# A decoder trunk on one core: projections of the next head pair placed between the attention steps of the present one, the two heads of a pair in halves of the TensorE array

## The chip, the cores and the metric

The kernel runs on one core of one Trainium2 chip, as one program. A core has TensorE (matmuls, results in PSUM, 8 banks of 128 x 512 words), VectorE, ScalarE, GpSimd and a DMA queue on SyncE. The metric is the time of one execution on the device in microseconds (us); the shown time is a median of three runs.

## The reference, cut to what matters

512 tokens, width 1024, two layers. Each layer is a mixer (three kinds of causal attention, six heads of 64 each), merged by gates, and then a feed-forward part with 16384 experts and product keys. Only the mixer's first half is touched:

```python
xn = rms_norm(h, norm1_g[l])
proj = xn @ w_in                       # qa ka va  qb kb vb  f  qc kc vc  gates
# branch 0 (A): dilated windows: the three patterns are one softmax with a mask of log counts
# branch 1 (B): softmax(q.k / 8 + cum[t] - cum[s]) over s <= t,  cum = cumsum(log_sigmoid(f + b))
# branch 2 (C): window of 128, 6 query heads on 2 key heads, a sink in the denominator
oa, ob, oc = attention of each branch, per head
merged = sum over branches of sigmoid(gate_b) * (o_b @ w_br_b)
h = h + merged @ w_out
```

Attention works in blocks of 128 queries; a query block `qi` sees the key blocks `blocks(br, qi)`: 1, 2, 3, 4 of them in branches 0 and 1, and 1, 2, 2, 2 in branch 2.

## The kernel before, in words

**Streams and splits.** All weights come as chunks of 128 x 2048 words (1 MB) through two slots: a load (L325), ScalarE copies the high part (`split_hi`, L458) and VectorE subtracts the rest (`split_lo`, L743), and TensorE multiplies high by high, high by low and low by high (`product`, L1153 to L1155). `ahead(p, s)` on both engines means the split of the chunk after this one. A slot is split again only when TensorE has used it up (`w_used`).

**Order of a layer's mixer.** Normalise and transpose x; two chunks for the keys and values that branch 2 shares (`kv`, evicted by L504); then three head pairs `hp`, one after the other; then the merge: 24 chunks, each with 8 products for a gate and 3 for a branch; then the output projection.

**One head pair.** Four chunks give the projections of the pair: 64 products, each 3 matmuls over 452 columns. Between them VectorE rotates queries and keys (L816 to L822), and VectorE and ScalarE make the forget gate's logarithm (L517, L518; it needs another ScalarE table than the exponential) and the cumulated sum. Then 24 transposes (L1227) give `qT` and `kT`. `qT` is kept once per head, with the other head's 64 rows zero (set by GpSimd once in a layer), so that logits are matmuls of all 128 rows. GpSimd copies the pair's shared keys and values into `proj` (L410).

**The attention of a pair.** 24 units (branch, head, query block) in a pipeline written out by hand with four logit buffers. A unit: logits on TensorE (L1244; branch 1 adds L1246), mask and maximum on VectorE (L877), negated maximum (L882, L884), exponential on ScalarE (L545), reciprocal and normalisation on VectorE (L893, L894), transposes of the probabilities on TensorE (L1257), copy to SBUF on ScalarE (L557), values on TensorE (L1267), which form 128 output columns of which one head's 64 are kept. TensorE issues logits three units ahead; the transposes have two banks. Outputs are split in high and low (L563, L796) for each branch and head. All engines execute in order, with waits on semaphores.

## Time and profile before

| | us |
|---|---|
| median of 3 runs (3490.7 to 3494.0) | 3491.5 |
| the profiled execution | 3496.1 |
| its span in the trace | 3494.3 |

| stage of layer 0 | us from the span's start |
|---|---|
| x, shared keys and values | 0 to 38.4 |
| three head pairs | 38.4 to 279.6 |
| merge, output projection | 280 to about 484 |
| the feed-forward part | to about 1750 |

Layer 1 repeats this. The page gives busy shares of the whole span; what an engine waits for is read from the chain of waits and from the timeline of a stage.

### The profile page before, as it was taken

What the parts mean: (1) busy time and instruction counts of PE and PEld (TensorE: products, weight loads), DVE (VectorE), ACT (ScalarE), POOL (GpSimd) and SP (SyncE); (2) the same over time, 40 slices, a digit from 0 to 9 for tenths busy, and PEclk for the clock granted to TensorE, in tenths of its full rate; (3) what the DMA queues carried; (4) which work ended last, traced back from release to release, by engine and by line L of the source; (5) the groups of instructions that cost most, each with busy time, mean ns of one, the idle gap of its engine ahead of it and who ended that gap; (6) DMA issues with size and microseconds to landing.
All of it is one profiled execution on the core that took longest, in us unless ns stands there. A gap on an engine that the chain in (4) does not pass through costs nothing.

```text
span 3494.3 us, 53359 instructions
## 1 busy us (share of the span) xinstructions
PE 3421.8 (98%) x18272; PEld 3003.5 (86%) x18272; DVE 2677.5 (77%) x5087; ACT 1642.3 (47%) x2531; POOL 1109.9 (32%) x701
## 2 busy tenths in 40 slices
PE   7999999999999999999999999999999999999998
PEld 6888778999999987777788887789999998878777
DVE  5665448999997688888866644399999967888887
ACT  5664333457775333333356643334577753333333
POOL 1000003673333354444200000137633333544442
PEclk9999999999999999999999999999999999999999
DMA  4112322569999999999721133225799999999996
GB/s 148 48 48 106 135 102 85 178 232 369 370 369 388 367 376 360 370 374 378 293 85 49 48 121 132 104 83 190 259 371 367 364 388 366 385 357 380 374 369 248
DMA packets 226906, 885.59 MB, mean 253 GB/s; under 512 B 20752, under 2 KB 70304, under 8 KB 178000
## 3 DMA queue, kind: packets, MB, share of 16 engines
q1 hardware_dynamic: 121136, 478.99, 37.1%
q0 software_dynamic: 83648, 304.09, 23.1%
q10 hardware_dynamic: 21984, 100.94, 7.1%
q8 instruction: 54, 0.88, 0.1%
q14 instruction: 84, 0.69, 0.1%
HBM read 781.17 MB, written 102.76 MB: 253 GB/s over the span
## 4 chain that ended last, share of the span: by engine, by line
PE 75%; DVE 10%; DMA 6%; issue 5%; ACT 4%; ACTq 0%; DVEq 0%; SPq 0%
PE bank L1153 18%; PE bank L1155 17%; PE bank L1154 17%; PE bank L1420 13%; DMA raw<-in_stream 5%; PE bank L1384 5%; DVE lo L743 3%; DVE h L1055 3%; PE bank L1267 2%; DVE act_in L1106 1%; ACT hi L458 1%; ACT w_hi L706 1%; PE bank L1244 1%; PE bank L1257 1%; PE bank L1333 1%
## 5 line engine op out<-in xcount | busy, mean ns | idle before, releaser
L743 DVE TENSOR_TENSOR lo<-raw,hi 128x2048 fp32r<-128x2048 f32 x304 | 696.5, 2291 | 335.6 <-ACT hi L458 333.4
L1153 PE MATMUL bank<-xT_hi,hi 128*128 128x352 f32 (+1 forms) x2688 | 924.7, 344 | 4.5 <-DVE lo L743 2.4
L1154 PE MATMUL bank<-xT_lo,hi 128*128 128x352 f32 (+1 forms) x2688 | 910.9, 339 | 0.0
L1155 PE MATMUL bank<-xT_hi,lo 128*128 128x352 f32 (+1 forms) x2688 | 910.4, 339 | 0.0
L458 ACT ACTIVATE hi<-raw 128x2048 fp32r<-128x2048 f32 x324 | 620.0, 1914 | 408.8 <-PE bank L1420 172.4
L1420 PE MATMUL bank<-hi,w_hi 128*128 128x512 f32 x1536 | 612.6, 399 | 10.8 <-DVE w_lo L1108 10.4
L1420 PE MATMUL bank<-hi,w_lo 128*128 128x512 f32 x1536 | 608.8, 396 | 0.0
L1420 PE MATMUL bank<-lo,w_hi 128*128 128x512 f32 x1536 | 608.8, 396 | 0.0
L1153 PEld LDWEIGHTS bank<-xT_hi,hi 128*128 128x128 f32 x2688 | 506.2, 188 | 34.6 <-issue 7.2
L447 POOL DMA_INDIRECT rows<-in_v_rows,ids x256 | 387.4, 1513 | 467.0 <-DVE h L1055 383.8
L1155 PEld LDWEIGHTS bank<-xT_hi,lo 128*128 128x128 f32 x2688 | 505.4, 188 | 25.9
L1154 PEld LDWEIGHTS bank<-xT_lo,hi 128*128 128x128 f32 x2688 | 505.8, 188 | 24.3
L447 POOL DMA_INDIRECT rows<-in_u_rows,ids x256 | 327.4, 1279 | 536.7 <-DVE act_row L1052 450.3
L1420 PEld LDWEIGHTS bank<-hi,w_hi 128*128 128x128 f32 x1536 | 289.2, 188 | 94.2 <-DVE w_lo L1108 25.5
L1420 PEld LDWEIGHTS bank<-hi,w_lo 128*128 128x128 f32 x1536 | 289.3, 188 | 70.5
L1420 PEld LDWEIGHTS bank<-lo,w_hi 128*128 128x128 f32 x1536 | 289.4, 188 | 68.9
L1055 DVE SCALAR_TENSOR_TENSOR h<-rows,w_row,h 128x1024 f32<-128x1024 f32 x256 | 328.3, 1283 | 16.6
L706 ACT ACTIVATE w_hi<-act_in 128x768 fp32r<-128x768 f32 x128 | 108.4, 847 | 487.7 <-DVE act_in L1106 484.4
L1052 DVE CUSTOM_DVE_ANT_0 rows<-rows,x_row 128x1024 f32<-128x1024 f32 x256 | 300.4, 1221 | 0.1
L1108 DVE TENSOR_TENSOR w_lo<-act_in,w_hi 128x768 fp32r<-128x768 f32 x128 | 122.7, 958 | 126.6 <-ACT w_hi L706 126.6
L435 POOL TENSOR_TENSOR lo<-raw,hi 128x1024 fp32r<-128x1024 f32 x64 | 201.0, 3154 | 45.1 <-ACT hi L638 45.0
L1089 DVE TENSOR_SCALAR onehot<-iota_sb,idx1T,gT 128x128 f32<-128x128 f32 x768 | 202.9, 365 | 0.0
(213 smaller groups left out, 4608.2 us busy)
## 6 DMA issues: line engine op xcount, KB each, us to landing
raw<-in_stream SPq DMA_DIRECT2D x356, 1024.0 KB
act_d<-act_s ACTq DMA_DIRECT2D x128, 384.0 KB
gate_d<-gate_s ACTq DMA_DIRECT2D x24, 2048.0 KB
act_in<-act_d SPq DMA_DIRECT2D x128, 384.0 KB
gate_in<-gate_d SPq DMA_DIRECT2D x28, 1536.0 KB
gate_in<-gate_d SPq DMA_DIRECT2D x16, 384.0 KB
rows<-in_u_rows,ids POOLq DMA_INDIRECT x256
rows<-in_v_rows,ids POOLq DMA_INDIRECT x256
```

What stands on the lines that cost most here:

```text
L435: pool.tensor_tensor(lo[s][:, half], raw[s][:, half], hi[s][:, half].bitcast(F32), ALU.subtract).then_inc(lo_done if i else lo0_done, 1)
L447: pool.indirect_dma_start(rows[:, N % NR], None, a["u_rows" if n < E + P else "v_rows"], bass.IndirectOffsetOnAxis(which, 0)).then_inc(row ...
L458: act.activation(hi[s][:], raw[s][:], ACT.Copy).then_inc(hi_done, 1)
L743: dve.tensor_tensor(lo[s][:], raw[s][:], hi[s][:].bitcast(F32), ALU.subtract).then_inc(lo_done, 1)
L1052: last = dve.tensor_tensor_reduce(row, row, x_row[:], 1.0, 0.0, ALU.mult, ALU.add, act_row[:, k])
L1055: last = dve.scalar_tensor_tensor(out=h[:, ROWED], in0=row, scalar=w_row[:, k], in1=h[:, ROWED], op0=ALU.mult, op1=ALU.add)
L1089: last = dve.tensor_scalar(o[:, r, 0], iota[:], idx1T[:, t], gT[:, t], ALU.is_equal, ALU.mult)
L1153: pe.matmul(dst, a_[0], b_[0], start=first, stop=False)
L1154: pe.matmul(dst, a_[0], b_[1], start=False, stop=False)
L1155: return pe.matmul(dst, a_[1], b_[0], start=False, stop=last)
L1384: last = pe.matmul(ps[4 + slot][:, tile(r)], o[:, 1], o[:, 0], start=True, stop=True)
L1420: last = pe.matmul(ps[2 * tt + nh][:], wp[:, s, i, tile(tt)], v[vp][:, 2 * i + nh], start=False, stop=False)
```

## The change

- The projections of pair 0 run alone as before. The 64 products of the next pair are then dealt out over 25 slots that stand between the attention steps of the present pair (`slot`, `proj_groups`), two or three products each. In the last pair the slots carry 16 gate products of the merge's first two chunks instead (`gate_groups`).
- The two heads of a pair are one step: 12 steps `w` instead of 24 units. Each head's logits are a matmul of its 64 rows of `qT` and `kT`, head 0 in the upper rows of the array and head 1 in the lower, into two banks; values use 64 columns of the array for each head, into one bank. `qT` is kept once for both; the zeroing of halves is gone.
- Banks: logits 0 and 1, transposes one bank (2) for both heads in turn, outputs one bank (3), projections 4 to 7. Two logit buffers per head instead of four for all. TensorE issues logits two steps ahead.
- ScalarE and VectorE do the splits of the next pair's chunks at steps 0, 3, 6 and 9, evictions at 4 to 6 and 10 to 12, the rotation (in halves of two query tiles) at 7, 8, 10, 11, the forget gate at 1 to 4. Negated maxima, reciprocals and sink terms are done once for both heads, and the output's high and low parts for both heads at once.
- Before pair 0's projections TensorE now waits for the shared keys and values to be evicted (`kv_ev`; before: ahead of the third chunk). GpSimd copies the values of branches 0 and 1 into `v_ab`; shared keys and values are read in place.

```diff
+STEPS = [(br, qi) for br in (0, 2, 1) for qi in range(NT)]
+NW = len(STEPS)
+TURN_BANK, O_BANK, PROJ_BANK = 2, 3, 4
+PRE_SLOTS = 3
+SLOTS = PRE_SLOTS + 2 * NW
+FILLED = SLOTS - 2
+PROJ_GROUPS = PROJ_CHUNKS * NT * NK // 2
+EARLY_GATES = 2
+SPLIT_AT = {0: 0, 3: 1, 6: 2, 9: 3}
+EVICT_AT = {4: [(0, 0), (0, 1)], 5: [(0, 2)], 6: [(0, 3)], 10: [(1, 0)], 11: [(1, 1)], 12: [(1, 2), (1, 3)]}
+ROPE_AT = (7, 8, 10, 11)
+F_EXP_AT, F_SUM_AT, CUM_HI_AT, CUM_LO_AT = 1, 2, 3, 4
```

ScalarE's steps:

```diff
+                    for w in range(NW + 1):
+                        if w < NW:
+                            br, qi = STEPS[w]
+                            nk = len(blocks(br, qi)) * P
+                            act.wait_ge(lg_done, NW * b + w + 1)
+                            for hh in range(2):
+                                u = 2 * w + hh
+                                done = act.activation(lg[:, w % 2, hh, 0:nk], lg[:, w % 2, hh, 0:nk], ACT.Exp,
+                                                      bias=nmx[:, u:u + 1], accum_out=den[:, u:u + 1])
...
+                        if w == F_EXP_AT:
                             link = Chain(act, f_act, 2 * b, 2)
                             act.wait_ge(f_x, b + 1)
                             link(act.activation(fg[:, 1], fg[:, 1], ACT.Exp))
                             link(act.activation(fg[:, 1], fg[:, 1], ACT.Ln, bias=one[0:2, 0:1]))
...
+                        for hh in range(2 if w > 0 else 0):
+                            v = w - 1
+                            nk = len(blocks(*STEPS[v])) * P
+                            act.wait_ge(tr_done, 2 * (NW * b + v) + hh + 1)
+                            if hh == 0:
+                                act.wait_ge(pv_done, NW * b + v + 1)
+                            act.activation(pT[:, hh, 0:nk], ps[TURN_BANK][:, 0:nk], ACT.Copy).then_inc(pt_done, 1)
+                            if hh == 0:
+                                tasks(hp, w, last)
+                        if w == 0:
+                            tasks(hp, w, last)
+                        if not last:
+                            for r, tt in EVICT_AT.get(w, ()):
+                                proj_evict(b + 1, r, tt)
```

VectorE's steps:

```diff
+                    for w in range(NW):
...
+                        for hh in range(2):
+                            u = 2 * w + hh
+                            if w >= 2:
+                                dve.wait_ge(tr_done, 2 * (NW * b + w - 2) + hh + 1)
+                            wait_alone(dve, s_ps, 2 * (NW * b + w) + hh + 1, dve_passed)
+                            dve.tensor_tensor_reduce(lg[:, w % 2, hh, 0:nk], ps[hh][:, 0:nk], m, SCALE, -3e38, ALU.add, ALU.max,
+                                                     mx[:, u:u + 1]).then_inc(mx_link, 1)
+                        dve.wait_ge(mx_link, 2 * (NW * b + w) + 2)
...
+                        if w in SPLIT_AT and not last:
+                            c = SPLIT_AT[w]
+                            ahead(lp + KV_CHUNKS // 2 + (hp + 1) * (PROJ_CHUNKS // 2) + c // 2, c % 2)
+                        if w == 0 and last:
+                            ahead(lp + P_MRG, 0)
...
+                        dve.wait_ge(ex_done, NW * b + w + 1)
...
+                        den_chain(dve.reciprocal(rden[:, pair], den[:, pair]))
+                        for hh in range(2):
+                            u = 2 * w + hh
+                            dve.tensor_scalar(lg[:, w % 2, hh, 0:nk], lg[:, w % 2, hh, 0:nk], rden[:, u:u + 1], None,
                                               ALU.mult).then_inc(pn_done, 1)
+                        if w >= NT + 1 and (w - NT - 1) % NT == 0:
+                            o_split_lo(b, hp, (w - NT - 1) // NT)
```

TensorE's logits, values and order:

```diff
+                        for hh in range(2):
+                            of = slice(hh * DH, hh * DH + DH)
+                            done = pe.matmul(dst[hh], qT[br][of, tile(qi)], kT[br][of, keys], start=True, stop=br != 1)
...
+                                done = pe.matmul(ps[O_BANK][of, tile(qi)], v, pT[:, hh, tile(n)],
+                                                 start=n == 0, stop=n == len(bl) - 1)
...
+                    def slot(i):
+
+                        total = EARLY_GATES * NK if last else PROJ_GROUPS
+                        first, end = (min(total, -(-total * n // FILLED)) for n in (i, i + 1))
+                        if last:
+                            gate_groups(first, end, b)
+                        else:
+                            proj_groups(hp + 1, first, end, b)
+
+                    logits(0)
+                    slot(0)
+                    slot(1)
+                    logits(1)
+                    slot(2)
+                    for w in range(NW):
+                        if w >= 1:
+                            values(w - 1)
+                        turn(w, 0)
+                        slot(PRE_SLOTS + 2 * w)
+                        turn(w, 1)
+                        if w + 2 < NW:
+                            logits(w + 2)
+                        slot(PRE_SLOTS + 2 * w + 1)
+                    values(NW - 1)
+
+                pe.wait_ge(kv_ev, l + 1)
+                proj_groups(0, 0, PROJ_GROUPS)
+                for hp in range(HP):
+                    attention(hp, hp == HP - 1)
```

`turn(w, 1)` waits for the copy of `turn(w, 0)` out of the one bank (`pt_done`), `values(w)` for both copies, and the first values of a branch for the low part of the branch before (`o_lo`).

## Rows read from the trace of the kernel before

**Rows 1.** The page: busy time of each engine, and the chain that ended last, by engine.

```profile
PE 3421.8 (98%) x18272; PEld 3003.5 (86%) x18272; DVE 2677.5 (77%) x5087; ACT 1642.3 (47%) x2531; POOL 1109.9 (32%) x701
...
PE 75%; DVE 10%; DMA 6%; issue 5%; ACT 4%; ACTq 0%; DVEq 0%; SPq 0%
```

**Rows 2.** Windows of layer 0: busy us, instructions, PE clock, DMA.

```profile
core 0: us, PE busy (x) PEld busy (x) DVE busy (x) ACT busy (x) POOL busy (x), PEclk, DMA share, GB/s
...
38.40:78.54 40.14, 39.98 (x198) 36.18 (x197) 22.21 (x20) 17.57 (x23) 3.14 (x2) 1.00 0.37 130
...
78.54:119.03 40.49, 37.50 (x243) 29.15 (x242) 32.18 (x137) 31.86 (x94) 0.00 (x0) 1.00 0.00 1
...
280.00:372.00 92.00, 92.00 (x401) 74.82 (x400) 42.73 (x35) 35.04 (x30) 0.00 (x0) 1.00 0.37 134
```

**Rows 3.** The chain, start and us: last value products of four pairs.

```profile
118.12 1.16 PE bank L1267 x8
...
198.39 1.16 PE bank L1267 x8
...
1853.06 1.16 PE bank L1267 x8
...
1933.74 1.16 PE bank L1267 x8
```

**Rows 4.** The chain, first pair: spacing of attention matmuls.

```profile
89.50 0.44 PE bank L1257 x4
...
90.61 0.86 PE bank L1244 x2
...
91.58 0.89 PE bank L1267 x8
...
113.81 0.23 PE bank L1246
```

**Rows 5.** Timeline, start and us: one unit of four blocks on VectorE and ScalarE.

```profile
114.96 0.15 DVE L884 TENSOR_SCALAR nmx<-mx 128x1 f32<-128x1 f32 x1
...
115.15 0.72 ACT L545 ACTIVATE lg<-lg,nmx 128x512 f32<-128x512 f32 x1 [0.69 <-DVE nmx L884]
...
116.00 0.16 DVE L893 RECIPROCAL rden<-den 128x1 f32<-128x1 f32 x1 [0.36 <-ACT lg L545]
...
116.20 0.48 DVE L894 TENSOR_SCALAR lg<-lg,rden 128x512 f32<-128x512 f32 x1
```

**Rows 6.** Groups by form, 38.4 to 280 us: count, busy us, mean ns, idle.

```profile
L545 ACT ACTIVATE lg<-lg,nmx 128x512 f32<-128x512 f32 x12 | 8.7, 722 | 7.4 <-DVE nmx L884 7.4
...
L545 ACT ACTIVATE lg<-lg,nmx 128x128 f32<-128x128 f32 x18 | 7.2, 398 | 0.6 <-DVE nmx L882 0.5
...
L877 DVE CUSTOM_DVE_ANT_0 lg<-bank,mask_b 128x512 f32<-128x512 f32 x6 | 4.2, 692 | 2.3 <-PE bank L1257 2.3
...
L877 DVE CUSTOM_DVE_ANT_0 lg<-bank,mask_b 128x128 f32<-128x128 f32 x6 | 1.7, 285 | 0.0
...
L557 ACT ACTIVATE pT<-bank 128x512 f32<-128x512 f32 x12 | 7.1, 593 | 1.6 <-PE bank L1257 1.5
```

**Rows 7.** Timeline: one weight chunk split, high half and low half.

```profile
121.31 1.92 ACT L458 ACTIVATE hi<-raw 128x2048 fp32r<-128x2048 f32 x1
...
123.26 2.29 DVE L743 TENSOR_TENSOR lo<-raw,hi 128x2048 fp32r<-128x2048 f32 x1 [2.41 <-ACT hi L458]
```

**Rows 8.** Timeline: the forget gate's logarithm and its table.

```profile
71.22 1.28 ACT L518 ACT_TABLE_LOAD   x1
...
72.51 0.72 ACT L518 ACTIVATE fg<-fg,one 2x512 f32<-2x512 f32 x1
```

**Rows 9.** Timeline: the shared keys and values leave their banks.

```profile
38.60 2.32 ACT L504 ACTIVATE kv<-bank 128x256 f32<-128x256 f32 x8 [3.78 <-PE bank L1155]
```

**Rows 10.** Windows at the start of the span, as rows 2.

```profile
21.70:24.40 2.70, 0.00 (x0) 0.00 (x0) 2.70 (x3) 2.70 (x6) 0.00 (x0) 1.00 0.00 0
...
26.80:30.20 3.40, 3.40 (x18) 3.40 (x17) 3.40 (x5) 0.98 (x1) 0.93 (x2) 0.51 0.32 135
```

More of the change, by code:

```diff
@@ L106 @@
 FIRST_PAIR, REST_PAIR = 0, 8
-ZEROED = 7
 TWO_PI = 2 * np.pi
@@ L567, in _, with o_hi_split @@
+                def o_hi_split(b, hp, g):
+                    act.wait_ge(pv_done, NW * b + NT * g + NT + 1)
+                    act.activation(oT_hi[:, bass.ds(hp * 3 + STEPS[NT * g][0], 1), :].rearrange("p o t -> p (o t)"),
+                                   ps[O_BANK][:], ACT.Copy).then_inc(o_hi, 1)
+                with act.Fori(0, HP - 1) as hp:
+                    attention(hp, False)
+                attention(HP - 1, True)
+                for j in range(NK // M_BLOCKS):
                     for m in range(3 * M_BLOCKS):
@@ L902, in _ @@
+                with dve.Fori(0, HP - 1) as hp:
+                    attention(hp, False)
+                attention(HP - 1, True)
+                for j in range(NK // M_BLOCKS):
                     for m in range(3 * M_BLOCKS):
@@ new lines, in proj_groups @@
+                        if g % 16 == 0:
+                            take(lp + KV_CHUNKS // 2 + hp * (PROJ_CHUNKS // 2) + c // 2, s)
+                        if beside is not None and c == 0 and k == 0:
+                            bank_free(beside, tt)
+                        if c == 2 and k == 0:
+                            pe.wait_ge(proj_ev, 2 * NT * b + tt + 1)
+                        last = product(ps[PROJ_BANK + tt][:, 0:PROJ_COLS], at(xT, s * NK // 2 + k, tile(tt)),
+                                       at(chunk(s, PROJ_COLS, NK // 2), k), s == 0 and k == 0, s == 1 and k == 3)
@@ new lines, in proj_groups, with gate_groups @@
+                        if g % 16 == 15:
+                            last.then_inc(w_used, 1)
+                        elif s == 1 and k == 3:
+                            last.then_inc(proj_ps, 1)
+                def gate_groups(first, end, beside):
+                    for g in range(first, end):
+                        m, k = g // NK, g % NK
+                        if k == 0:
+                            take(lp + P_MRG, m)
+                            bank_free(beside, m)
+                        product(ps[4 + m][:], at(chunk(m, P, NK + HP), k), at(xT, k), k == 0, k == NK - 1)
@@ new lines, in logits, with turn @@
+                        for hh in range(2 if br == 1 else 0):
+                            pe.matmul(dst[hh], select[:, hh], cum[:, keys], start=False, stop=True).then_inc(s_ps, 1)
+                    def turn(w, hh):
+                        n = 2 * (NW * b + w) + hh
+                        pe.wait_ge(pn_done, n + 1)
+                        if w == hh == 0:
+                            pe.wait_ge(heads_dve, 3 * b + 2)
+                        else:
+                            pe.wait_ge(pt_done, n)
+                        for i in range(len(blocks(*STEPS[w]))):
+                            done = pe.transpose(ps[TURN_BANK][:, tile(i)], lg[:, w % 2, hh, tile(i)], ident[:])
+                        done.then_inc(tr_done, 1)
```

435 lines of the change are left out of this document (187 added, 248 removed).

## The prediction

> **What bounds the kernel now.** I read the page first, then windows by stage, then the chain and the timeline of one head pair. TensorE is busy 98% of the span and carries 75% of the chain [rows 1], so a gain must take work or idle time from TensorE. The change touches three head pairs and the start of the merge in each layer. Two successive pairs of layer 0 end 80.3 us apart, two of layer 1 80.7 [rows 3]. The window of pair 0 divides at 78.5: about 39.4 us of products (64 x 3 matmuls, 0.205 each), all of them dense, then 40.5 us of attention, in which neither VectorE (32) nor ScalarE (32) is full [rows 2]. What TensorE really needs there comes from spacings, because busy time counts the drain of a lone matmul. A transpose takes 0.11, a value product (two records) 0.22, a logits product 0.86 for 512 columns and its decay term 0.23 [rows 4]. A pair has 28 transposes of heads and gates and 54 of probabilities (9.0), 6912 logit columns (11.6), 2560 columns with decay (1.2) and 54 value products (12.0): 33.8 us. The pair's 80.3 less 39.4 and 33.8 leaves **7.1 us of idle TensorE**. That is all that better cover can bring, 43 us for six pairs. If both heads' matmuls ran at once, values would halve (6 us) and logits lose a quarter, since only the second record of head 0 and the first of head 1 can overlap (2.9): 8.9 a pair, 53 in all.
>
> **What the change adds: one ring.** Before, VectorE put the next unit's reduction ahead of waiting for an exponential, with four logit buffers. Now each step does, in order, two reductions, a negation, a wait for both exponentials, one reciprocal, two normalisations; the next reduction stands behind that wait. For four blocks: reductions 2 x 0.73, 0.19 to the exponential, 2 x 0.72, 0.32 to the first normalisation, 2 x 0.40: 4.2 us, from the starts in [rows 5] and the means in [rows 6], less 0.1 where neighbours overlap. One block gives 2.5 in the same way; two and three lie between (3.0, 3.6); the sink terms of branch 2 add 0.6. Twelve steps: 2 x 13.3 + 13.9 = **40.5 us** serial.
>
> Into that ring the change puts more, in the two pairs that carry projections. A split costs 1.95 on ScalarE and then 2.2 on VectorE [rows 7]; VectorE takes it before it waits for the exponential, ScalarE after a copy, so the whole 4.2 stands between exponential and normalisation at steps 0, 3, 6 and 9: 17.8 with the copies. The gate's logarithm (exponential 0.6, table 1.28, logarithm 0.72) [rows 8] now stands in ScalarE's queue at step 1, ahead of the copy that frees the one transpose bank; the way back to the exponential's table costs another 1.28, mostly waited for anyway. Low parts, sums and rotation not hidden by an exponential: about 3. VectorE starts 4.6 after the last values (low part 0.65, three head copies, two gate operations), and the last step needs 3.9 for two turns through one bank and its values. The ring alone: 4.6 + 40.5 + 17.8 + 4 + 3.9 = **71 us**. TensorE alone: 39.4 + 33.8 = 73 without overlap of the heads, 64 with. Two chains of nearly equal length with only two steps of look-ahead don't hide each other wholly.
>
> **Laid out step by step** from the end of the values before, with TensorE's order as the diff gives it and a group of three matmuls at 0.615, TensorE waits: 1.8 at the first transpose (it has 5 us of slots, the ring with the split takes 11); 3.4 at the second (the logarithm stands before its copy; one slot of 1.85 covers); 0.8 and 1.4 around the split at step 3, where the copy for the second head stands behind the next step's exponentials, which stand behind the late normalisation; 0.3 and 1.8 at step 6; 1.5 and 0.5 at step 9, where the values of branch 1 need the low part that VectorE does after the split; 1.2 in the last step, whose slots are empty. Sum 12.7: the pair takes 33.8 + 39.4 + 12.7 = **85.9 us**, if the halves of the array bring nothing, and 80.5 if they overlap as above (a part of the 8.9 turns into waits for the ring). No row shows a matmul in a part of the array. Nothing excludes a loss either: every step goes four times between shapes, and a last matmul shows 1.16 where spaced ones show 0.89 [rows 3, 4], so an emptied array costs at most 0.27, 13 us a pair for 48 changes. I take half of the overlap's gain: **83.2**.
>
> The Trainium skill ("TensorEngine Tiling (Array Packing)", Key Properties) says that different tiles can execute in parallel, and in the same list that changing the tiling mode drains the engine, which speaks against this order of steps. By the first alone a pair would take 80.5, by both about 84; no run here shows either yet.
>
> **The last pair of a layer** has 16 gate products of 3 x 0.23 (401 matmuls in the 92 us of the merge's window [rows 2]) in its slots, 11.0 us, and one split. TensorE needs 44.8, the ring 4.6 + 40.5 + 4.2 + 4 + 3.9 = 57. But now the look-ahead is the limit: logits of step w+2 stand behind the second transpose of w, that behind a copy, that behind the exponentials of w+1. From one exponential to the next but one this takes a copy (0.3 to 0.6) [rows 6], a transpose, the logits (0.4 to 2.2), reductions and exponentials; laid out it comes to 66.8, and 64 with overlap: **65.4**, against 40.9 before.
>
> **The smaller parts.** The wait for `kv_ev` ahead of pair 0's first product: before, TensorE went on while ScalarE evicted from 38.60 for 2.32 us [rows 9]. Nothing stands behind it: +2.5 a layer. VectorE's rotation of the shared keys moves with it and stays hidden. At the merge's start the gate products are gone that covered the third chunk's split: branch products of the two chunks take 4.2, sigmoid and split end at 7.1: +2.9, and -11.0 for the products moved. Removed memsets, GpSimd's copies and the lesser zero rows were on no chain; its new copy of the values (about 2 us) has 19 us. Loads (two in 10 us) are as many and have a step of slack.
>
> **The clock.** After 2.7 us without a matmul TensorE ran 3.4 us at half its clock, that is 1.2 GHz, some 2.4 us later [rows 10]. The waits of 3.4 us in two pairs, and two of over 4 us at the start of the last, may do that; a drop costs up to 1.7. I take about one in a layer: +1.5.
>
> **Sum.** A layer's pairs took 240.8. Now 39.4 + 2.5 + 2 x 83.2 + 65.4 + 2.9 - 11.0 + 1.5 = 267.1, +26.3; both layers +52.6. The span would be 3546.9 for 3494.3; the profiled execution (3496.1) lies 0.1% above the median of the runs, 3491.5, so I put the median at **3544 us**.
>
> **Rivals.** (1) *The tasks hide.* If splits and logarithm fell where engines wait anyway and the ring stayed at its own length, a pair would take 72 and the last 54: 39.4 + 2.5 + 144 + 54 + 2.9 - 11.0 = 231.8 a layer, 3473 in all, **faster**. It decides below 76 us a pair. For it: TensorE's products cover 3.2 us of each step. Against it: all four engines' orders are fixed, and the waits above follow from them. If tiles overlapped and all waits vanished too, the limit would be near 3395; hardly likely. Chance 0.19. (2) *Tiles cost.* No overlap and a drain of half of 0.27 at each change, a third of it in waits: 90 a pair, 71 the last, 3580. Chance 0.16. (3) *The gains meet the waits*: full overlap, and a third of the laid-out waits: some 75 a pair and 58 the last, 3493. Chance 0.07. That the shapes don't take effect as array parts is the no-overlap case, 63 us over: 3555, within the forecast. Forecast, 3515 to 3565: 0.58.
>
> **How the numbers follow.** A measurement of this kernel can tell 0.2% from no change, 7 us. The range takes in the forecast, (3) and most of (1) and (2): 3472 to 3588. Faster 0.20, within 0.2% 0.06, slower 0.74.
>
> **What would show it.** The start of the second attention should come some 83 us after the first; TensorE should idle 3 us before the second transpose, released by ScalarE's copy, with a table load ahead of it; VectorE should wait for ScalarE's high part at steps 0, 3, 6, 9; the last pair should take 60 to 70 us and TensorE be about two thirds busy in it; value products of two heads should be spaced by 0.11 to 0.22. I am wrong if a pair with projections takes under 77 us, or if the last pair's steps run at 3.4 us as before; then the ring overlaps in a way that I haven't seen.

## The result and the profile after

The changed kernel takes **3558.1 us** (median of four runs, 3555.0 to 3562.6) against 3491.1 on the same chip: a ratio of 1.0195, 95% interval 1.0177 to 1.0212, so 67 us slower. Its profiled execution took 3557.6, with a span of 3555.8, 61.5 more than the span of before.

First the page of the changed kernel: busy time and the chain that ended last.

```profile
PE 3411.0 (96%) x18272; PEld 2948.2 (83%) x18272; DVE 2650.8 (75%) x4974; ACT 1603.2 (45%) x2463; POOL 1103.8 (31%) x683
...
PE 73%; DVE 11%; issue 7%; ACT 6%; DMA 3%; ACTq 0%; DVEq 0%; SPq 0%
```

As many matmuls as in [rows 1] are busy for 11 us less, though the span is 61 longer: the busy share falls from 98% to 96%, and what is new is idle TensorE.

The stages of layer 0, on the timeline of TensorE (start, duration, line, [idle before]):

```profile
40.14 0.47 PE L1186 MATMUL bank<-hi,xT_hi 128*128 128x452 f32 x1 [2.50 <-ACT kv L504]
...
81.06 1.47 PE L1279 MATMUL bank<-ident_sb,proj 128*128 128x128 f32 x12
...
165.87 1.53 PE L1279 MATMUL bank<-ident_sb,proj 128*128 128x128 f32 x12
...
251.74 1.53 PE L1279 MATMUL bank<-ident_sb,proj 128*128 128x128 f32 x12
...
319.93 1.09 PE L1332 MATMUL bank<-pT,v_ab 128*64 128x128 f32 x16 [0.69 <-ACT pT L560]
...
328.39 0.79 PE L1186 MATMUL bank<-xT_hi,hi 128*128 128x512 f32 x1 [2.96 <-DVE lo L764]
```

Attention begins with the head transposes (L1279). The pairs that carry projections take 84.8 and 85.9 us (80.3 before, [rows 3]), the last one 69.3 to the end of its values at 321.0. In layer 1 they take 84.8, 84.9 and 71.5. Attention of layer 0 ended at 279.6 before, so it ends 41.4 later. Layer 1's head transposes come 33.7 later (1846.84 for 1813.11), and up to 2.5 of that is the second layer's own wait for `kv_ev`: from the merge on 10.2 is given back, 11.0 less 3.0 of it by the moved gate products and the wait at 328.39. The matmuls from 328.97 on are 0.43 apart, at half clock; those from 331.9 on are 0.23 apart.

Windows of the same stages (length, busy us and instructions by engine, granted clock):

```profile
81.06:166.40 85.34, 74.76 (x444) 55.73 (x443) 45.53 (x130) 42.69 (x101) 1.32 (x2) 0.96 0.14 50
166.40:251.74 85.34, 74.35 (x437) 54.71 (x434) 45.86 (x131) 42.13 (x100) 0.76 (x1) 0.94 0.14 50
251.74:320.90 69.16, 48.16 (x296) 28.50 (x294) 33.01 (x116) 32.41 (x88) 1.04 (x1) 0.88 0.05 16
320.90:412.00 91.10, 88.14 (x379) 71.49 (x376) 43.45 (x37) 34.23 (x30) 0.00 (x0) 0.98 0.37 127
```

TensorE is idle for some 11 us in each of the first two, where it was idle 3.0 in the 40.5 of [rows 2], and for 21 in the last pair. The granted clock was 1.00 in all of this stage before. A mean of 0.96, 0.94 and 0.88 between levels of 1.0 and 0.5 is 7, 10 and 17 us at half clock (1.2 GHz). In layer 1 the means are 0.98, 0.98 and 0.82: 3, 3 and 26 us.

What TensorE waits for in the first of these stretches, then in the last (engine, line waited for: us in total, times, longest):

```profile
PE bank L1314 <- ACT pT L560: 4.6, 4, 1.6
PE bank L1314 <- DVE lg L919: 3.4, 3, 2.0
PE bank L1332 <- DVE oT_lo L815: 1.8, 1, 1.8
PE bank L1332 <- ACT pT L560: 0.7, 1, 0.7
...
PE bank L1314 <- ACT pT L560: 13.0, 11, 3.4
PE bank L1314 <- DVE lg L919: 5.9, 2, 4.7
```

L1314 is the transpose of the probabilities. It waits either for the normalisation (L919) or for the copy (L560) that frees the one transpose bank for the second head: 8.0 us with projections, 18.9 in the last pair. L1332 are the value products; with their waits the first stretch has 10.5 us.

### The profile page after: what moved, and what is told of

Its sections match the earlier page's. It is cut to its first block, busy times and chain, and to the rows that moved or that the text cites. A ratio compares the mean times of both kernels' runs of the same rounds, so it can differ in the third digit from the quotient of the medians.

```text
span 3555.8 us, 52652 instructions
## 1 busy us (share of the span) xinstructions
PE 3411.0 (96%) x18272; PEld 2948.2 (83%) x18272; DVE 2650.8 (75%) x4974; ACT 1603.2 (45%) x2463; POOL 1103.8 (31%) x683
## 4 chain that ended last, share of the span: by engine, by line
PE 73%; DVE 11%; issue 7%; ACT 6%; DMA 3%; ACTq 0%; DVEq 0%; SPq 0%
PE bank L1186 17%; PE bank L1187 17%; PE bank L1188 17%; PE bank L1503 14%; PE bank L1467 5%; DVE h L1087 4%; DVE lo L764 3%; DMA raw<-in_stream 3%; ACT hi L458 2%; DVE act_in L1138 1%; ACT w_hi L727 1%; PE bank L1314 1%; PE bank L1332 1%; ACT lg L537 1%; PE bank L1300 1%
## 5 line engine op out<-in xcount | busy, mean ns | idle before, releaser
L1188 PE MATMUL bank<-xT_hi,lo 128*128 128x352 f32 (+1 forms) x2688 | 912.0, 339 | 0.0
L447 POOL DMA_INDIRECT rows<-in_v_rows,ids x256 | 395.0, 1543 | 451.9 <-DVE h L1087 362.2
L1188 PEld LDWEIGHTS bank<-xT_hi,lo 128*128 128x128 f32 x2688 | 507.0, 189 | 26.8
```

What stands on the lines that cost most here:

```text
L447: pool.indirect_dma_start(rows[:, N % NR], None, a["u_rows" if n < E + P else "v_rows"], bass.IndirectOffsetOnAxis(which, 0)).then_inc(row ...
L1188: return pe.matmul(dst, a_[1], b_[0], start=False, stop=last)
```

## The experiments

Each ratio is to the kernel before on the same chip (3489 to 3490 us); the time beside it is a median, and differences are to the 3558.1 of the change, whose own chip had 3491.1 for the kernel before. Two stage times recur, both of layer 0: *pairs* are the distances between the transposes of the shared keys in successive pairs (84.9 and 85.9 in the changed kernel), *last* is from there to the end of the layer's values (67.9).

| kernel | us | pairs | last |
|---|---|---|---|
| changed | 3558.1 | 84.9, 85.9 | 67.9 |
| full shapes | 3577.3 | 88.1, 86.5 | 71.7 |
| reductions ahead | 3576.0 | 87.5, 86.1 | 74.5 |
| logarithm late | 3545.2 | 83.1, 82.4 | 69.2 |
| products early | 3546.7 | 83.2, 82.2 | 68.0 |
| filler in the last pair | 3551.1 | 84.9, 84.9 | 65.9 |
| no interleaving | 3676.4 | 115.4, 114.2 | 68.7 |
| the same, full shapes | 3664.5 | 110.1, 109.4 | 71.3 |
| split late | 3571.4 | 88.7, 88.7 | 68.9 |
| all mended | 3560.1 | 88.0, 88.5 | 64.4 |
| mended, split kept | 3541.4 | 82.2, 83.5 | 66.9 |

**1. The heads' matmuls in full shapes.**

```diff
-    done = pe.matmul(dst[hh], qT[br][of, tile(qi)], kT[br][of, keys], start=True, stop=br != 1)
+    done = pe.matmul(dst[hh], qT[br][:, tile(qi)], kT[br][:, keys], start=True, stop=br != 1)
...
-    v = v_ab[:, kb, br * P + hh * DH:br * P + hh * DH + DH]
-    done = pe.matmul(ps[O_BANK][of, tile(qi)], v, pT[:, hh, tile(n)],
-                     start=n == 0, stop=n == len(bl) - 1)
+    v = v_ab[:, kb, br * P:br * P + P]
+    done = pe.matmul(ps[O_BANK][:, tile(qi)], v, pT[:, hh, tile(n)],
+                     start=n == 0 and hh == 0, stop=n == len(bl) - 1 and hh == 1)
```

> The changed kernel with its order kept, but logits and values as full 128 x 128 array shapes (same count and columns). It computes something else: each head's logits are the sum over both heads, and the values of both heads are added. In the trace of the changed kernel four value products of a head pair are spaced 0.216 us per key block plus 0.16 once, where full shapes take 0.44 per block: the parts save TensorE about 7.8 us a pair. Theory (the ring of reductions, exponentials and normalisations sets the pace, the parts' gain goes mostly into waits): a pair with projections goes from 85.3 to 88 to 90, the last from 69 to about 71, the median from 3558 to 3575 to 3590. Rival 1 (TensorE sets the pace and all of the gain counts): +47, 3605. Rival 2 (changing the shape of the array costs more than the overlap gives): at or under 3558.

Measured: 3577.3, ratio 1.026 (1.0243 to 1.0277), 19 us more, as the first theory has it. Each head's logits and values hold the other head's as well here, so only times can be compared. What the parts save is read from the same step in the changed kernel and in this one, where a row's next row starts when the array is free:

```profile
161.00 0.36 PE L1188 MATMUL bank<-hi,xT_lo 128*128 128x452 f32 x1
161.29 0.88 PE L1332 MATMUL bank<-pT,v_ab 128*64 128x128 f32 x12
162.10 0.66 PE L1314 MATMUL bank<-ident_sb,lg 128*128 128x128 f32 x4
...
164.84 1.09 PE L1332 MATMUL bank<-pT,v_ab 128*64 128x128 f32 x16 [0.69 <-ACT pT L560]
```

```profile
162.34 0.37 PE L1188 MATMUL bank<-hi,xT_lo 128*128 128x452 f32 x1
162.54 1.50 PE L1332 MATMUL bank<-pT,v_ab 128*128 128x128 f32 x12
163.88 0.60 PE L1314 MATMUL bank<-ident_sb,lg 128*128 128x128 f32 x4
```

Four more value records (a key block of both heads) take 0.22: 0.81 for twelve up to the next row, 1.03 for sixteen (the next row there is L1279 at 165.87). In full shape a block of *one* head takes that ([rows 4]). So the two heads overlap wholly. But the visit to the other shape costs time, and not only inside it: the product before it (L1188) holds the array for 0.29 and not 0.20, and the transposes behind it last 0.06 longer. From the start of the record before a visit to the start of the second record behind it, at full clock and without a wait, these are the times (at the starts in brackets):

| visit, for both heads | changed | full shapes |
|---|---|---|
| logits, one key block (84.21, 83.47) | 0.94 | 0.76 |
| logits, two (118.22, 117.87) | 1.14 | 1.18 |
| logits, four (104.72, 104.32) | 1.57 | 2.03 |
| values, one (126.17, 126.52) | 0.83 | 0.76 |
| values, two (107.20, 107.27) | 1.05 | 1.20 |
| values, three (161.29, 162.54) | 1.26 | 1.65 |
| values, four (120.88, 120.58) | 1.41 | 2.02 |

Half of the full-shape time should be saved; what is missing is 0.29 for each visit with values and about 0.4 for most with logits. With one key block the parts lose time, and for logits two blocks are about even. Over the 12 steps of a pair the whole saving, by the sum of such visits, is about 4 us, where whole overlap alone would give 11.8. A second way gives much the same: in layer 1, where both kernels have 3.4 us at half clock in each pair with projections, such a pair is 3.3 us longer in full shapes and waits 1.2 less, 4.5 together. So six pairs save TensorE 23 to 27 us. The runs show 19; TensorE's waits in the six pairs are 87 us in the changed kernel and 79 in this one, so the rest went into waits.

**2. VectorE's reductions one step ahead.** The forecast made VectorE's order the heart of the ring, so this should have opened it.

```diff
-                    for w in range(NW):
+                    def reductions(w):
...
+                    reductions(0)
+                    for w in range(NW):
...
+                        if w + 1 < NW:
+                            reductions(w + 1)
                         dve.wait_ge(ex_done, NW * b + w + 1)
```

> The changed kernel, but VectorE takes the reductions and the negation of step w+1 before it waits for the exponentials of step w; nothing else is moved. Theory (ring): the exponential of the next step is no longer behind the normalisation; the last pair goes from 69 to 58 to 63 us, a pair with projections from 85.3 to 79 to 82, the median to 3515 to 3530. Rival (the interleaving as such, or the shapes of the array, cost the time): within 5 us of 3558.

Measured: 3576.0, ratio 1.0249 (1.0232 to 1.0266): 18 us *slower*. VectorE's waits in the last pair of this kernel and one row of its timeline show what the edit did (half clock is part of the price too: 27 us of layer 0's last pair here, 17 in the changed kernel):

```profile
DVE lg L885 <- PE bank L1310: 18.6, 6, 5.7
DVE lg L885 <- PE bank L1314: 13.9, 4, 5.1
```

```profile
271.66 0.56 DVE L885 CUSTOM_DVE_ANT_0 lg<-bank,mask_a 128x384 f32<-128x384 f32 x1 [5.75 <-PE bank L1310]
```

The reduction (L885) of step w+1 needs its logits, which TensorE issues behind the second transpose of w-1. The normalisation of w, already due, now stands behind that wait. Taking the reductions out of VectorE's order did not open the ring. What holds it can be read in the changed kernel itself, in a step of its last pair:

```profile
292.82 0.41 PE L1314 MATMUL bank<-ident_sb,lg 128*128 128x128 f32 x2 [1.34 <-ACT pT L560]
293.16 0.70 PE L1300 MATMUL bank<-kT,qT 64*128 64x256 f32 x4
294.03 0.42 DVE L885 CUSTOM_DVE_ANT_0 lg<-bank,mask_c 128x256 f32<-128x256 f32 x1 [0.58 <-issue]
295.24 0.51 ACT L537 ACTIVATE lg<-lg,nmx 128x256 f32<-128x256 f32 x1 [1.59 <-DVE esink L891]
296.33 0.36 ACT L560 ACTIVATE pT<-bank 128x256 f32<-128x256 f32 x1
296.83 0.41 PE L1314 MATMUL bank<-ident_sb,lg 128*128 128x128 f32 x2 [0.42 <-ACT pT L560]
```

Second transpose, logits of two steps on (L1300), their reductions (L885), their exponentials (L537), the copy that frees the one transpose bank and stands behind them on ScalarE (L560), and the second transpose of the next step: 4.0 us, each behind the one before. For the reduction the profile names no engine (issue), but in three steps running it starts 0.87 after the logits (284.87, 289.15 and 293.16). VectorE had finished its normalisations by 293.5 and was idle for 0.58 before the reduction, so its order does not bind here; the loop through the look-ahead and the one bank does. My theory named the right kind of queueing and the wrong member of it.

**3. The logarithm behind the copies of step 1.**

```diff
-                        if w == F_EXP_AT:
-                            link = Chain(act, f_act, 2 * b, 2)
-                            act.wait_ge(f_x, b + 1)
-                            link(act.activation(fg[:, 1], fg[:, 1], ACT.Exp))
-                            link(act.activation(fg[:, 1], fg[:, 1], ACT.Ln, bias=one[0:2, 0:1]))
-                            link.end()
                         if w == CUM_HI_AT:
...
                             tasks(hp, w, last)
+                        if w == F_EXP_AT:
+                            link = Chain(act, f_act, 2 * b, 2)
...
```

> The changed kernel, but ScalarE makes the forget gate's exponential and logarithm behind the two copies of step 1 and not ahead of them. Theory: TensorE's wait for ScalarE's copy before the second transpose (1.6 us in a pair with projections, 3.4 in the last) goes; the logarithm and two table loads then stand before the exponential of step 2, which has about 2 us of slack. Median 5 to 12 us under 3558. Rival (the wait only moves to step 2): within 3 us of 3558, with the same sum of TensorE's waits at the next transposes.

Measured: 3545.2, ratio 1.016 (1.0143 to 1.0177), 13 us faster. The edit acts on all six pairs: those of layer 0 change by -1.8, -3.4 and +1.3 us, those of layer 1 by -2.9, -3.0 and -3.7. ScalarE's timeline in the changed kernel:

```profile
94.69 0.61 ACT L545 ACTIVATE fg<-fg 2x512 f32<-2x512 f32 x1
95.32 1.28 ACT L546 ACT_TABLE_LOAD   x1
96.61 0.72 ACT L546 ACTIVATE fg<-fg,one 2x512 f32<-2x512 f32 x1
97.50 0.28 ACT L560 ACTIVATE pT<-bank 128x128 f32<-128x128 f32 x1 [0.17 <-ACT fg L546]
```

and in this one, with TensorE's second transpose:

```profile
93.51 0.25 ACT L554 ACTIVATE pT<-bank 128x128 f32<-128x128 f32 x1
93.91 0.30 PE L1314 MATMUL bank<-ident_sb,lg 128*128 128x128 f32 x1 [0.29 <-ACT pT L554]
94.25 0.28 ACT L554 ACTIVATE pT<-bank 128x128 f32<-128x128 f32 x1 [0.48 <-PE bank L1314]
94.42 0.61 ACT L562 ACTIVATE fg<-fg 2x512 f32<-2x512 f32 x1
```

The first copy comes at 93.5 instead of 97.5 (1.2 of this because the stage's transposes begin earlier here, at 81.20 for 82.37). It had stood behind 2.6 us of gate work. The wait before the second transpose is 0.29 and was 1.60; this shows the forecast's cause for it.

**4. More products ahead of the second transpose** (17 instead of 11; the same 64 in all, dealt out otherwise).

```diff
-                            proj_groups(hp + 1, first, end, b)
+                            ends = [0, 4, 8, 13, 17, 18, 20, 21, 23, 24, 26, 28, 30, 33, 36, 38, 41, 43, 46, 48, 51, 53, 56, 58, 61, 64, 64, 64]
+                            proj_groups(hp + 1, ends[i], ends[i + 1], b)
```

> The changed kernel, but the 64 products of the next pair are dealt out with 17 instead of 11 ahead of the second transpose and 47 instead of 53 behind it. Theory: TensorE's waits of 2.0 and 1.6 us before the first two transposes of a pair with projections go, and the pair shortens by 2 to 5 us in four pairs, since TensorE has less to do behind: median 8 to 20 us under 3558. Rival (the ring alone sets the length of the pair): the waits only move to later transposes, within 4 us of 3558.

Measured: 3546.7, ratio 1.0161 (1.0144 to 1.0178), 11.5 faster, as expected: the same waits can be covered as well as removed.

**5. Filler in the last pair.**

```diff
                             gate_groups(first, end, b)
+                            w, second = divmod(i - PRE_SLOTS, 2)
+                            extra = 3 if i == 2 else 2 if i in (3, 5) else 1 if w >= 2 and not second else 0
+                            if i == 2:
+                                pe.wait_ge(heads_act, 3 * b + 3)
+                            for _ in range(extra):
+                                product(ps[7][:], at(chunk(0, P, NK + HP), 0), at(xT, 0), True, True)
```

> The changed kernel with more work: in the last pair of each layer TensorE does 17 further products (3 full matmuls of 512 columns each, 0.69 us at full clock, 11.7 us in all) into a bank that nobody reads: three before the first transpose, two each before the next two second transposes, one in each later step. No result uses them. In the changed kernel the clock's mean in the last pair is 0.88 and 0.82 in the two layers. Clock theory (waits of 3 to 5 us and matmuls in parts of the array lower the clock, and that lengthens the last pair and the merge's start): the mean clock there rises to 0.95 or more and the pair goes from 69 to 63 to 67 us in spite of the work, the median 5 to 12 us under 3558. Ring theory alone: the pair stays at 69 to 72, the median at 3556 to 3566.

Measured: 3551.1, ratio 1.0174 (1.0157 to 1.0191): 11.7 us of added work in each layer, and a median 7 us lower. That alone is hardly clear of the noise, since the runs (3547.7 to 3561.1) overlap with those of the change (3555.0 to 3562.6). The last pairs are clearer: 2.0 us shorter in layer 0 and 3.6 in layer 1, in spite of the work. The window of layer 0's last pair, and under it three windows of the changed kernel around its two longest waits there:

```profile
250.10:317.20 67.10, 56.63 (x346) 36.72 (x345) 33.01 (x116) 32.37 (x88) 1.05 (x1) 0.97 0.05 17
```

```profile
256.00:260.00 4.00, 1.72 (x9) 0.81 (x7) 1.27 (x6) 2.36 (x5) 0.00 (x0) 1.00 0.00 0
...
260.00:264.00 4.00, 0.90 (x3) 0.81 (x4) 3.58 (x9) 0.32 (x1) 0.00 (x0) 0.51 0.13 16
...
272.00:276.00 4.00, 3.44 (x12) 1.17 (x10) 2.40 (x5) 1.81 (x6) 0.00 (x0) 0.50 0.00 0
```

Waits of 4.73 and 3.41 us (at 263.10 and 268.26) come with half clock from 260 to beyond 276, and then the logits and transposes on the loop take twice as long. The filler has 0.97 where the change has 0.88 (0.97 for 0.82 in layer 1), and TensorE waits 8.4 us at L1314 and not 18.9.

**6. No interleaving: the new steps alone.** Slots are empty in the first two pairs, and the next pair's projections come as one block behind the attention, with their splits and rotation. A second kernel is the same with full shapes as in experiment 1.

```diff
...
                         else:
-                            proj_groups(hp + 1, first, end, b)
+                            pass
...
                     values(NW - 1)
+                    if not last:
+                        proj_groups(hp + 1, 0, PROJ_GROUPS, b)
```

> The changed kernel without the interleaving: the slots of the first two pairs are empty, and the next pair's projections, splits, evictions and rotation follow the attention as a block, as they do for pair 0. The steps in pairs, the parts of the array and the last pair with its gate products stay. Theory (the new steps are slower than the old units, and the interleaving wins back part of it): such a pair takes 39.4 + 58 to 64 = 97 to 103 us instead of 85.3, the median 3600 to 3635. Rival (the tasks of the interleaving in the queues of ScalarE and VectorE are what costs): a pair at 80 to 85, the median at or under 3558.

> As e8 (slots of the first two pairs empty, projections as a block behind the attention), and logits and values as full shapes as in e1 (so the values computed are those of both heads together). e8 took 115 us for such a pair at a clock of 0.62 in its attention, not the 97 to 103 laid out. Clock theory (parts of the array on their own, without full matmuls between them, lower the clock): with full shapes the clock's mean is above 0.85 in the attention and a pair takes 97 to 106 us; that is the length of the ring of steps, 58 to 66, against 40.9 for the old units; median 3600 to 3650. Rival (waits alone lower the clock): the clock stays near 0.62 and the median at or above 3676.

Measured: 3676.4, ratio 1.0533 (1.0515 to 1.0551), and with full shapes 3664.5, ratio 1.0497 (1.0476 to 1.0518). Windows of the first attention, in the first kernel (80 to 165 holds also the start of the block) and then in the second:

```profile
80.00:165.00 85.00, 60.06 (x291) 38.30 (x290) 33.55 (x116) 34.11 (x90) 1.03 (x1) 0.62 0.04 14
```

```profile
81.06:152.00 70.94, 45.08 (x248) 34.12 (x247) 31.00 (x114) 31.65 (x88) 1.04 (x1) 0.86 0.00 1
```

The new attention takes 74 us by itself, and 71 in full shapes, where the old units took 40.5. Of the 71 TensorE waits 26, where it waited 3; the half clock is part of the rest. Both kernels came out longer than expected; a clock of 0.62 was in no theory of the first, and 0.86 in the second is what its clock theory asked for, though its pair of 110 us is longer than the 97 to 106 that went with it. A pair is 115 us long against 85 with the projections in the slots. In full shapes it is 110 against 87 (experiment 1): **the interleaving itself earns some 22 us a pair by filling waits, and some 29 where it also holds the clock up**, and the steps it was bought with lose more. That the kernel with *less* TensorE work is the slower one here, by 12 us at 0.62 against 0.86, says that parts of the array cost clock where no full products stand between.

**7. The array's parts in the kernel before.** First logits in rows and values in columns; then the columns alone. In its order of one head after the other nothing can overlap, so work stays the same.

```diff
-  last = pe.matmul(dst, qT[br][hh][:, tile(qi)], kT[br][:, keys], start=True, stop=br != 1)
+  of = slice(hh * DH, hh * DH + DH)
+  last = pe.matmul(dst, qT[br][hh][of, tile(qi)], kT[br][of, keys], start=True, stop=br != 1)
...
-  last = pe.matmul(ps[g % 2][:, tile(qi)], proj[:, kb, V_COL[br]:V_COL[br] + P],
+  last = pe.matmul(ps[g % 2][of, tile(qi)], proj[:, kb, V_COL[br] + hh * DH:V_COL[br] + hh * DH + DH],
```

> The kernel before, with only the array shapes changed: logits from the 64 rows of their head, values into the 64 columns of their head. Units of one head follow each other there, so nothing can overlap; what is left is the change of shape four times a unit. If each visit to another shape costs about 0.16 to 0.2 us, as the trace of the changed kernel suggests, 24 units add 8 us a pair less what idle time hides: 80.3 goes to 84 to 88, the median from 3491 to 3515 to 3540. Rival (a change of shape is free): within 5 us of 3491.

> The kernel before with only the values in the 64 columns of their head; logits in the full shape. With logits and values in parts it took 3688, and TensorE, busy throughout, ran at half its clock from the second quarter of each attention to its end. If the lower clock comes with the share of the array in use, columns alone (about a third of the matmul time) lower it less or not at all: 3500 to 3560, mean clock in the attention above 0.8. If any visit to a part of the array brings it, the clock is at half as before, and the time above 3620.

Measured: 3688.1, ratio 1.0551 (1.0513 to 1.0588), far outside what either theory allowed, and for columns alone 3507.9, ratio 1.0053 (1.0033 to 1.0073). Windows of the first kernel, and of the second:

```profile
78.54:120.00 41.46, 39.90 (x136) 23.32 (x135) 21.08 (x89) 20.74 (x61) 0.00 (x0) 0.60 0.00 1
120.00:145.00 25.00, 25.00 (x69) 13.42 (x67) 9.60 (x42) 8.81 (x26) 0.00 (x0) 0.50 0.00 0
154.00:160.00 6.00, 6.00 (x31) 5.51 (x31) 2.70 (x2) 3.79 (x3) 1.17 (x2) 1.00 0.00 0
```

```profile
78.54:120.00 41.46, 39.48 (x226) 26.55 (x225) 32.03 (x136) 31.59 (x93) 0.00 (x0) 1.00 0.00 1
```

With rows and columns TensorE's records fill 25.00 of 25.00 us and the granted clock is 0.50, and it is 1.00 again once the next pair's full products run. With columns alone it stays 1.00, and the kernel is 18 us longer, 3 a pair. Two visits with one key block, read as in the table of experiment 1, take 0.88 (at 99.61) where the kernel before takes 0.55 (at 97.85); 24 visits at 0.33 would make 8 us, so the larger part of them falls into time that TensorE lost anyway. Whether rows alone would lower the clock was not tried, nor whether it is the smaller part of the array in use or the stops between shapes that lowers it.

**8. The split late.** On VectorE behind normalisation and low part, on ScalarE behind both copies.

```diff
-                            if hh == 0:
+                            if hh == 1:
                                 tasks(hp, w, last)
...
-                        if w in SPLIT_AT and not last:
-                            c = SPLIT_AT[w]
-                            ahead(lp + KV_CHUNKS // 2 + (hp + 1) * (PROJ_CHUNKS // 2) + c // 2, c % 2)
...
                             o_split_lo(b, hp, (w - NT - 1) // NT)
+                        if w in SPLIT_AT and not last:
+                            c = SPLIT_AT[w]
+                            ahead(lp + KV_CHUNKS // 2 + (hp + 1) * (PROJ_CHUNKS // 2) + c // 2, c % 2)
...
```

> The changed kernel, but the splits of the next chunks stand behind the normalisations (and the output's low part) of their step on VectorE, and behind both copies on ScalarE. Theory (the split between exponential and normalisation makes TensorE wait): the waits of 2.0, 0.85 and 0.54 us for the normalisation and of 1.8 for the output's low part go from each pair with projections, some of it coming back as a later reduction; a pair shortens by 2 to 4 us, the last by about 2, the median is 12 to 22 us under 3558. Rival (the ring is as long in either order): within 4 us of 3558.

Measured: 3571.4, ratio 1.0231 (1.0214 to 1.0248), 13 *slower*. TensorE's waits in the first pair (80.1 to 168.8), and its second transpose on the timeline:

```profile
PE bank L1314 <- ACT pT L560: 12.2, 5, 4.7
PE bank L1332 <- ACT pT L560: 0.7, 1, 0.7
```

```profile
96.37 0.45 PE L1314 MATMUL bank<-ident_sb,lg 128*128 128x128 f32 x1 [4.73 <-ACT pT L560]
```

The waits for normalisation (3.4) and low part (1.8) are gone, as meant. But the split still stands before *something*: now before the next step's reductions, so its exponentials, so the copy that stands behind them. That wait was 1.60 and is 4.73. All in all TensorE waits 2.4 us more in this pair, which is 3.8 us longer; it also has 14 us at half clock for 7. This agrees with the loop of experiment 2: a split costs more inside it than beside it. How much of the 13 us the clock has was not separated.

**9. All edits together, with and without that of experiment 8.** Experiments 3, 4 and 5, no wait for `kv_ev`, and first also the late split.

> The changed kernel with the edits of e3 (logarithm behind the copies), e5 (filling products in the last pair), e6 (more products early) and e11 (splits late) together, and without the wait for kv_ev ahead of pair 0's products (2.5 us idle a layer in the trace). The measured gains so far are 13, 7 and 11.5, the last two give 5 and 12 to 22 by theory: if they add, 3500 to 3512; if they remove the same waits, 3515 to 3530. In no case is it expected under the 3490 of the kernel before.

> The changed kernel with the logarithm behind the copies of step 1, 17 rather than 11 products before the second transpose, 17 extra full products in the last pair's slots, and no wait for kv_ev ahead of pair 0's products; the split stays where the change has it. Alone the first three were worth 13, 11.5 and 7 us; the wait's 2.5 a layer is 5. If each acts on its own wait, the sum is 36.5: about 3521 us. If the two edits of step 1 (logarithm, products) cover the same wait, one of them is worth little: 3530 to 3535. If the shifted waits come back elsewhere, as they did in the kernel that also moved the split, 3550 or more: then it was not the split that made that one slow. In no case does it come under the 3489 of the kernel before, since the last pair still runs at the ring's pace.

Measured: 3560.1 (ratio 1.0189, 1.0169 to 1.0209), no better than the change; without the late split 3541.4 (ratio 1.015, 1.0133 to 1.0167), 16.7 better. So the late split alone costs 19 in this company. But 16.7 is not the 36.5 of the sum, nor quite the 23 to 28 for two edits on one wait: the pairs are 82.2 and 83.5, no shorter than with either edit of step 1 alone. What both cover is one wait, worth 12 to 13 once. Nor was the wait for `kv_ev` worth its 2.5 a layer. It is gone, but pair 0's products now wait for the low part of a weight chunk:

```profile
48.85 0.47 PE L1186 MATMUL bank<-hi,xT_hi 128*128 128x452 f32 x1 [1.79 <-DVE lo L764]
```

From the last product of the shared keys to the head transposes layer 1 takes 41.3 us here and 41.9 in the changed kernel: 0.5 a layer is gained. That attention begins at 78.40 instead of 81.06 in layer 0 is for the most part the clock: 42 to 45 is at half clock in the changed kernel, which makes its 64 products 1.6 us longer than in layer 1.

## Where the prediction was right and where not

- **The direction and the size** held: +52.6 forecast, +67 measured, 3558 in a range of 3472 to 3588. In the spans it is 26.3 a layer against 30.8.
- **The wait for `kv_ev`**: +2.5 a layer forecast, a wait of 2.50 at 40.14 measured. Its size is right, its price is not shown to be: without it 0.5 a layer comes back (experiment 9), since the next chunk's low part is not ready.
- **The merge's start**: +2.9 forecast, 2.96 at 328.39. The merge as a whole came out about 2 us cheaper than -11.0 and +2.9 make it; what else shrank was not traced.
- **The pairs with projections**: 83.2 forecast, 84.8 to 85.9 measured in the two layers. Waits of 12.7 were laid out; TensorE waits 10.5 and 11.0 us in layer 0 and 12.1 twice in layer 1. Part of the miss is the clock, 3 to 10 us of each such pair at half clock where the sum had one drop of 3.4 in a whole layer. Even so TensorE's own work must have been more than 33.8 + 39.4 less the saving, by an estimated 2 us a pair (from the full-shape pairs of layer 1: 88.2, less 10.9 of waits and up to 1.7 for 3.4 us at half clock, is over 75 and not 73.2); where it lies was not traced.
- **The waits laid out**: forecast 1.8 and 3.4 at the first and second transpose. Layer 1 has 1.96 and 3.13, nearly that:

```profile
1863.68 0.30 PE L1314 MATMUL bank<-ident_sb,lg 128*128 128x128 f32 x1 [3.13 <-ACT pT L560]
```

  Layer 0 has 1.98 and 1.60, and there the products between the two transposes ran at half clock and filled more of the time. The cause of the second, the logarithm ahead of the copy, is shown by experiment 3; that slots could cover it, by experiment 4. The one for the low part at step 9, 1.5 forecast, is 1.8.
- **The ring** was the wrong step of the reasoning. I put the limit in VectorE's order (reductions behind the wait for exponentials), which gave 4.6 + 40.5 + 4 + 3.9 = 53 us without the splits, and added the splits' 17.8 to it. Experiment 6 has those steps without the splits at 71 us, and experiments 2 and 8 changed that order and both kernels became slower. What holds the steps is the look-ahead, which the forecast had named only for the last pair: second transpose through one bank, behind a copy, behind the next exponentials, with the logits of two steps on behind it. The step in experiment 2 shows it closed, 4.0 us for two key blocks with a sink where the ring had 3.6. That the pairs with projections came out close all the same is partly luck, since that loop is hidden there for the most part by the products. Whether the one bank or the look-ahead of two is the root is *argued*, not shown: a second transpose bank was not tried, though the kernels of experiment 6 leave banks 4 to 7 free in the attention of the first two pairs.
- **The last pair**: 65.4 forecast, 69.3 and 71.5 measured. The chain was right (waits of 4.73 for the normalisation and 3.41 for the copy), and the clock is the likely difference, with 17 and 26 us at half clock. With 0.97 for 0.88 the pair is 2 us shorter in spite of 11.7 us more work.
- **The clock** was the mis-sized term: +1.5 a layer, one drop of 3.4 us. A layer has some 33 us at half clock in its pairs (7, 10 and 17 in layer 0; 3, 3 and 26 in layer 1). The condition taken from [rows 10], 2.7 us without a matmul, was too strict: in layer 0's first pair the clock falls right after the wait of 1.98, and again after that of 1.60.

```profile
90.00:93.00 3.00, 1.02 (x6) 0.63 (x5) 2.96 (x5) 0.00 (x0) 0.00 (x0) 0.98 0.00 0
93.00:96.00 3.00, 3.00 (x9) 2.39 (x8) 1.40 (x8) 2.29 (x6) 0.00 (x0) 0.50 0.87 295
```

  Nor does one wait decide it: the 2.50 for `kv_ev` is followed by half clock in layer 0 (42 to 45) and by full clock in layer 1. Experiment 5 shows what the clock takes in the last pairs: 2.0 and 3.6 us come back although work was added.
- **The halves of the array**: the forecast took 4.45 us of work from a pair and 2.7 from its length. Experiment 1 gives about 4 of work, and 3.2, 0.7, 3.3 and 3.3 in the lengths of the four pairs with projections. This is right in size and luck in the making: "half of the overlap's gain" was a middle taken between bounds; the overlap was whole (11.8 and not 8.9, since I let only the second record of head 0 meet the first of head 1), and 24 visits at 0.3 to 0.4 took 8 of it back, more than the "at most 0.27" for an emptied array. The Trainium skill ("TensorEngine Tiling (Array Packing)", Key Properties) states both parallel tiles and a drain at a change of mode. This trace agrees with both: whole overlap, and 0.29 and about 0.4 for each visit.
- **The profiled execution**: I took the median 0.1% under it, after the one pair of numbers of before; the changed kernel's lies at its median (3557.6, 3558.1). The forecast put the median 2.9 under its span, it lies 2.3 over it: 5 of the 14 us missed. The other 9 are in the span.
- **The rivals**: (1), that the tasks hide, needed pairs below 76; they take 85. (3) needed 75. (2), a pair of 90 through drains without overlap, fails on experiment 1: the heads overlap, and the full shapes are slower. That the visits cost was right in it.

## What to carry to other kernels

Before two units of a pipeline are merged into one step, follow the buffer with the fewest copies around its loop (here one transpose bank: exponential, copy, transpose, next logits) and count what stands in each queue ahead of its members; a task moved out of one place of that loop into another gains nothing. Interleaving dense products was worth 22 to 29 us a pair and should be bought without shortening the look-ahead. Put two small matmuls side by side in the array only where they are long enough to pay for the visit: here logits of one key block lost 0.17 us, and those of four won 0.46. Give a stretch of small, waiting matmuls enough dense work to hold the clock: added work can then make it shorter.

## What the runs showed of the hardware

- Two heads in halves of the array overlapped wholly, by columns as by rows: 0.22 us per key block for both where one took 0.22. Each visit between full-shape matmuls cost 0.29 for values and about 0.4 for logits.
- Logits in 64 rows and values in 64 columns, one head after the other, brought the granted clock from 1.00 to 0.60 and then 0.50 in a stretch in which TensorE's records fill 25.00 of 25.00 us; columns alone left it at 1.00. The new steps without dense products between them gave 0.62, and 0.86 in full shapes.
- 17 extra products, 11.7 us of work, raised the last pair's clock from 0.88 to 0.97 and shortened it by 2 us (in layer 1 from 0.82 to 0.97, by 3.6 us).
- The granted clock fell to half after waits of 1.98 and 1.60 us in layer 0's first pair, and the same wait of 2.50 us was followed by half clock in one layer and by full clock in the other.
